# Sample attention of a hybrid decoder layer: page products of two key heads joined into one of 128 value columns

## The reference, cut to what matters

```
logits = jnp.einsum('btgrd,btkgd->btgrk', qg, ks).astype(F32) * (d ** -0.5)
logits = jnp.where(valid[:, :, None, None, :], logits, -jnp.inf)
p = jax.nn.softmax(logits, axis=-1).astype(vs.dtype)
o = jnp.einsum('btgrk,btkgd->btgrd', p, vs)
```

## Time and profile before

| what | value |
|---|---|
| median of the runs | 3233.22 us |
| the profiled execution | 3229.58 us |
| its span, first to last instruction | 3227.8 us |
| TensorE matmul busy | 2907.8 us, 90% of the span, 18215 instructions |
| TensorE weight loads busy | 2785.1 us, 86% |
| VectorE / ScalarE / GpSimd busy | 1545.5 / 711.8 / 564.0 us |
| mean granted TensorE clock | 0.919 of 2.4 GHz |
| page products of the samples (L1738) | 512 records, 46.4 us busy |

### The profile page before, as it was taken

The page is one execution under the profiler, slowest core; times in us unless marked ns, Lnnn a source line. Parts: engine busy times, 40 slices in busy tenths (PEclk is TensorE's granted clock), DMA queues, the critical chain, the costliest instruction groups (busy, mean ns, idle before and its releaser), DMA issues. The chain is left out here.

```text
span 3227.8 us, 48861 instructions
## 1 busy us (share of the span) xinstructions
PE 2907.8 (90%) x18215; PEld 2785.1 (86%) x18215; DVE 1545.5 (48%) x3330; ACT 711.8 (22%) x1381; POOL 564.0 (17%) x332
## 2 busy tenths in 40 slices
PE   8999999999478987799989966665998999999998
PEld 7999999999468975799968965555997999999998
DVE  5332222333685316899942757775625332223333
ACT  5111111112322125222211443432004111111111
POOL 0222111210111112122222210112100212112220
PEclk9999999999799777899995987667998999999999
DMA  3111111111112211233344222123401211111211
GB/s 120 52 53 52 39 39 39 56 41 40 62 59 88 65 33 33 80 120 125 105 127 113 51 84 94 54 61 119 122 27 59 62 43 52 39 39 39 65 33 55
DMA packets 239293, 213.04 MB, mean 66 GB/s; under 512 B 26978, under 2 KB 216578, under 8 KB 239042
## 3 DMA queue, kind: packets, MB, share of 16 engines
q1 hardware_dynamic: 230594, 182.58, 19.0%
q0 software_dynamic: 3968, 11.54, 1.3%
q10 hardware_dynamic: 4608, 17.30, 1.3%
HBM read 168.17 MB, written 43.21 MB: 65 GB/s over the span
## 5 line engine op out<-in xcount | busy, mean ns | idle before, releaser
L250 POOL TENSOR_TENSOR ff_wlo<-ff_raw,ff_whi 128x1024 fp32r<-128x1024 f32 x124 | 298.5, 2429 | 1206.4 <-ACT ff_whi L327 1205.5
L516 DVE TENSOR_TENSOR ff_prod<-ff_silu,ff_gu 128x384 f32<-128x384 f32 x132 | 68.7, 521 | 807.0 <-ACT ff_silu L332 807.0
L89 PE MATMUL ff_gu<-front_hhi,ff_whi 128*128 128x384 f32 (+1 forms) x1056 | 340.6, 323 | 2.1 <-DVE front_hlo L460 1.8
L89 PE MATMUL ff_dn<-ff_ahi,ff_whi 128*128 128x384 f32 (+1 forms) x1056 | 339.5, 322 | 0.9 <-DVE x_xT L529 0.9
L90 PE MATMUL ff_gu<-front_hlo,ff_whi 128*128 128x384 f32 (+1 forms) x1056 | 339.3, 321 | 0.0
L91 PE MATMUL ff_gu<-front_hhi,ff_wlo 128*128 128x384 f32 (+1 forms) x1056 | 339.2, 321 | 0.0
L89 PE MATMUL ff_gu<-rear_hhi,ff_whi 128*128 128x384 f32 (+1 forms) x1056 | 338.8, 321 | 0.0
L90 PE MATMUL ff_dn<-ff_alo,ff_whi 128*128 128x384 f32 (+1 forms) x1056 | 338.6, 321 | 0.0
L90 PE MATMUL ff_gu<-rear_hlo,ff_whi 128*128 128x384 f32 (+1 forms) x1056 | 338.5, 321 | 0.0
L91 PE MATMUL ff_gu<-rear_hhi,ff_wlo 128*128 128x384 f32 (+1 forms) x1056 | 338.5, 321 | 0.0
L91 PE MATMUL ff_dn<-ff_ahi,ff_wlo 128*128 128x384 f32 (+1 forms) x1056 | 338.5, 321 | 0.0
(11 more groups left out here) (322 smaller groups left out, 6252.8 us busy)
## 6 DMA issues: line engine op xcount, KB each, us to landing
ff_raw<-in_ffn_w_gate SPq DMA_DIRECT2D x44, 512.0 KB, 3.7
ff_raw<-in_ffn_w_up SPq DMA_DIRECT2D x44, 512.0 KB, 3.7
ff_raw<-in_ffn_w_down SPq DMA_DIRECT2D x44, 512.0 KB, 3.5
scratch_feat<-sel_stage ACTq DMA_DIRECT2D x32, 528.0 KB, 2.7
sel_raw<-in_w_in SPq DMA_DIRECT2D x28, 512.0 KB, 3.6
merge_gates<-scratch_feat SPq DMA_DIRECT2D x48, 176.0 KB, 2.5
tok_raw<-in_w_in SPq DMA_DIRECT2D x8, 1024.0 KB, 5.4
mix_pages<-in_cache_k SPq DMA_DIRECT2D x64, 128.0 KB, 2.1
```

What stands on the lines that cost most here:

```text
L89: nc.tensor.matmul(out, w_hi, x_hi, start=first, stop=False)
L250: nc.gpsimd.tensor_tensor(wlo[:, u, :], raw[:, u % RAW, :], whi[:, u, :], ALU.subtract).then_inc(w_lo_done, 1)
L516: nc.vector.tensor_tensor(prod[:, 0:w], act_out[:, b, 0:w], gu[:, b, 1, 0:w], ALU.mult).then_inc(prod_done, 1)
```

## The change

The two heads of a pair share one product. The stationary operand is the page's 128x128 block with both heads' value columns, the moving operand has 16 columns of probabilities (2 heads x 2 query heads x 4 tokens), and the output is 128 partitions by 16 columns. Of it two quarters are wanted: head g's 64 partitions with head g's columns. The other two quarters are products of one head's values with the other's probabilities, and nobody reads them. So `s_out_ps` grows from 64 to 128 columns for each G, `mix_pages` issues 16 products instead of 32 for a sequence, the product with the new values 2 instead of 4, and ScalarE's copy to `new_out` is done in 4 instructions of 64 partitions instead of 2 of 128 partitions. The number of semaphore increments stays as it was.

```diff
-        s_out_ps = big[:, 5 * 512:5 * 512 + 4 * NS].rearrange("p (G c) -> p G c", G=2)
+
+        s_out_ps = big[:, 5 * 512:5 * 512 + 2 * P].rearrange("p (G c) -> p G c", G=2)
...
             for G in range(2):
-                for g in range(2):
-                    r = slice(g * HD, (g + 1) * HD)
-                    kv = 2 * G + g
-                    nc.tensor.matmul(s_out_ps[r, G, :], v_new[:, kv * HD:(kv + 1) * HD],
-                                     new_probsT[:, G, r], start=(G == 0), stop=False)
+                nc.tensor.matmul(s_out_ps[:, G, :], v_new[:, G * P:(G + 1) * P], new_probsT[:, G, :], start=(G == 0), stop=False)
...
                 for G in range(2):
-                    for g in range(2):
-                        r = slice(g * HD, (g + 1) * HD)
-                        kv = 2 * G + g
-                        o = s_out_ps[r, G, :].rearrange("p (r t) -> p r t", t=NS)
-                        for n in range(PAGES):
-                            p = s_probsT[:, G, n, r].rearrange("p (r t) -> p r t", t=NS)
-                            last = nc.tensor.matmul(o[:, :, DT * b:DT * (b + 1)],
-                                                    pages[:, PAGES * (b % SLOTS) + n, kv * HD:(kv + 1) * HD],
-                                                    p[:, :, DT * b:DT * (b + 1)], start=False,
-                                                    stop=(b == DB - 1 and G == 1 and n == PAGES - 1))
+                    o = s_out_ps[:, G, :].rearrange("p (q t) -> p q t", t=NS)[:, :, DT * b:DT * (b + 1)]
+                    for n in range(PAGES):
+                        p = s_probsT[:, G, n, :].rearrange("p (q t) -> p q t", t=NS)[:, :, DT * b:DT * (b + 1)]
+                        last = nc.tensor.matmul(o, pages[:, PAGES * (b % SLOTS) + n, G * P:(G + 1) * P], p, start=False,
+                                                stop=(b == DB - 1 and G == 1 and n == PAGES - 1))
...
                     for G in range(2):
-                        nc.scalar.activation(new_out[:, 2 * G:2 * G + 2, :],
-                                             s_out_ps[:, G, :].rearrange("p (r t) -> p r t", t=NS), ACT.Copy
-                                             ).then_inc(s_kept, 1)
+                        for g in range(2):
+                            rows = slice(g * HD, (g + 1) * HD)
+                            kept = nc.scalar.activation(new_out[rows, 2 * G:2 * G + 2, :], s_out_ps[rows, G, g * HD:(g + 1) * HD
+                                                        ].rearrange("p (r t) -> p r t", t=NS), ACT.Copy)
+                        kept.then_inc(s_kept, 1)
```

## The result

The changed kernel took 3240.7 us, the median of 10 runs (3236.66 to 3244.41), against 3231.43 us for the kernel before, now also of 10 runs (3226.29 to 3237.77). The ratio is 1.003, with a 95% interval of 1.0021 to 1.0039: slower by 7 to 13 us. The profiled execution took 3236.66 us against 3229.58 before, 7.1 more.

What follows compares the result with a forecast made beforehand. TensorE's stream, mostly weight loads at half clock, was taken as the bound; +7.3 us for page products and seams and +0.1 for the new values' product gave +7.4 on 3233.2, so 3240.6 us, range 3231 to 3247.

Steps and rivals of the forecast that it cites:

- What bounds the stretch: Stretch with the page products: TensorE's own stream sets its length, mostly weight loads at half clock; added time reaches the end.
- The page products as they are: Before the change, a step's 64 narrow loads take 5.72 us, mostly about 106 ns apart.
- the price of the fast passages: Loads of different column halves run side by side at three changes of half per sequence, each worth 0.40 us.
- The wide block at 211 ns from L2537: Changed page products: 32 loads of 128 columns at 211 ns, 6.74 us a step, +8.2 us over eight steps.
- The seams: Load-stream holes before each step's first page product, 0.9 us in all, vanish when full-width blocks follow full-width ones.
- the lower bound: Page products with the holes taken back: +7.3 us, chosen over the dearer bound of +9.8 us.
- The product with the new values: Four loads of 128 columns replace eight, 0.46 us against 0.38: +0.1 us, or +0.5 at the lower clock.
- ScalarE's copies: Four copies instead of two take 0.2 to 0.5 us more, hidden by 0.89 us of ScalarE idle time.
- The hole at each change of the pair G: Rival: the stream stops 0.14 us before each run of 16 loads, 2.2 us more, 3245 us; 8 in 100.
- No change from equal columns: Rival: page products load 4096 columns either way, so a step stays about 5.7 us, 3232 to 3234; 12 in 100.
- The clock: Rival: full-width page products with 16 moving columns keep TensorE at 2.4 GHz, -21 us, 3212 us; 5 in 100.
- the moment of the rise: Clock rise after the last page product may shift by 3 us, -1.5 to +1.5 us; within the range, no separate chance.

## Why the prediction was right, step by step

*What bounds the stretch*: right. The 7.3 us that the page products grew by came out at the end all but undiminished: the stretch with them, the new values' product included, is 7.5 us longer, and the last store comes 7.3 later.

*The page products as they are, and the price of the fast passages*: right, and shown. 0.40 us for each change of the column half was read from one step; the kernels with 1 and 7 changes gave 0.40 each as well.

*The wide block at 211 ns from L2537*: right; 213 ns, and 6.83 us from first load to next foreign one where 6.74 was put down.

*The seams*: the lower bound was the right one. The 0.9 us of holes is 0.0 after. Both terms together were 7.3; measured are 0.91 x 8 = 7.3. The split was a little off: 1.11 a step for the products, 0.20 back for the seam, where I had 1.02 and 0.11. The wide load doesn't merely follow without a hole, it starts 0.12 us before L1773's last load ends. The two errors, 0.09 us a step each, cancel, and that is luck. Of the two sentences of the Trainium skill ("TensorEngine Tiling (Array Packing)", Key Properties) the trace agrees with both, and the second, parallel tiles, was the larger here: 3 x 0.40 us a step given up against 0.20 won.

*The product with the new values*: mis-sized. +0.1 us was put down; it is 0.64 against 0.38, +0.26. The four loads start 0.11 us apart, as priced, and the last one ends 0.52 us after the first began; but the next load doesn't follow at the same spacing, it starts 0.12 us behind that end. The blocks have 32 rows, so I take this for a seam, which I had priced only for the page products; no run tests it by itself.

*ScalarE's copies*: the price was wrong, the cover held. Four copies of 64 partitions take 0.91 us, not 0.5 to 0.8: they start 0.23 us apart where the two of 128 partitions started 0.12 apart. The idle time behind them shrank from 0.89 to 0.29 us, and TensorE's transposes (L1784) load from 1783.93 on, 0.36 behind the copies' end at 1783.57, where it was nearly 1 us. In the kernel with 128 moving columns, where these steps run at full clock, the cover was used up: L1784 waited 0.3 us for the same four copies.

*The rivals.* The hole at each change of the pair G did not come: the loads are evenly 213 ns apart. No change from equal columns: wrong here because the before side wasn't paid by columns in full. The rule of the Trainium skill ("TensorE: Matmul & The Clock Gate", section LDWEIGHTS), that the time goes by the columns, holds in proportion between a narrow and a wide load (107 and 213 ns); its figure, P / 1.2 ns, would give 53 and 107 ns, half of what these float32 loads took at 1.2 GHz, and it says nothing of loads side by side. The clock: it stayed at 0.50 with 16 columns and full width, as the following stretches of the changed kernel show (columns as in the earlier trace rows):

```profile
1717.01:1785.27 68.26, 67.85 (x320) 67.69 (x320) 9.40 (x48) 7.35 (x31) 9.82 (x14) 0.50 0.27 73
1785.27:1795.51 10.24, 9.53 (x68) 7.62 (x68) 8.63 (x33) 5.21 (x15) 3.40 (x2) 0.99 0.33 78
```

It rose 4.7 us behind the first load after the page products (1780.62), before 5.5. That fits the 0.3 us by which the rest of the attention is shorter: the moment of the rise played next to no part. Its price had been right in size: the kernel with 128 moving columns is 32 us below the changed one, 22 below the kernel before, for which I had 21.

*The total*: 3240.6 forecast, 3240.7 measured, but that closeness is partly luck. The forecast started from a median of 3 runs, 1.8 us above that of 10, and the difference of the medians is 9.3 us, where the traces account for 7.3; the interval, 6.8 to 12.6, holds both. By the traces' 7.3 us, 0.23%, slower by over 0.2% was as close a call as the 0.55 said.

## What to carry to other kernels

Where the weight loads set the time, count the columns that a series of small products loads, not the products: joining two narrow stationary blocks into one of double width saved no load time here (213 ns against twice 107), and gave up running them side by side. If blocks use only half the columns, alternate the halves product by product. And where TensorE is fully busy at half clock, try more moving columns for each load: here 128 in place of 16, most of their results thrown away, brought the clock up and paid for themselves, also in a version whose result is right.

## What was not expected of the hardware

The gain from a change of half is the same each time, 0.40 us from 1 to 7 changes in a step, about four loads of one half beside four of the other; it is used up when the halves alternate throughout, at 3.5 us for 64 loads. And 8 times the moving columns (16 to 128) took no longer per load at half clock (ten loads in 2.13 us in either kernel); with them the clock rose, and the same 32 loads took 3.57 us instead of 6.83. That it rises as well with two half-width streams of 64 columns (64 loads in 1.95 us) was open until it ran.
